# A weight chunk rounded one step later on ScalarE, in the projections of a two-block fp32 transformer kernel

## What is computed

```
h = rms_norm(x, norm1_w[l]) * (1.0 + scale1) + shift1
proj = (h.astype(dt) @ w_in[l]).astype(jnp.float32)
aq, ak, av, gq, gf, gi, gg = jnp.split(proj, split_at, axis=-1)
aq = rope_partial(rms_norm(aq.reshape(hs), q_norm_w[l]), positions)
ak = rope_partial(rms_norm(ak.reshape(hs), k_norm_w[l]), positions)
attn = dilated_attention(aq, ak, av.reshape(hs)).reshape(B, S, ATTN_WIDTH)
ho = hgrn2(gq, gf, gi, lb_all[l])
```

## Time and profile before

| | |
|---|---|
| three runs | 2380.01, 2382.95, 2384.18 us (median 2382.95) |
| the profiled execution | 2381.23 us, of which the profile's span is 2379.1 us |
| TensorE matmul busy | 2318.3 us (97% of the span) |
| TensorE weight load busy | 1934.7 us (81%) |
| VectorE busy | 1642.0 us (69%) |
| ScalarE busy | 1046.5 us (44%) |
| GpSimd busy | 59.8 us (3%) |
| mean granted TensorE clock | 0.992 of full speed |
| `w_hi` (L255) | 392 instructions, 1.917 us each |
| `w_lo` (L259) | 392 instructions, 2.290 us each |

### The profile page before, as it was taken

One profiled execution on the slowest core, in us unless ns is written; L12 is line 12 of the kernel. 1 busy time (PEld: TensorE's weight loads), 2 busy tenths in 40 slices (PEclk: granted clock), 3 DMA queues, 4 the chain that ended last, 5 costly groups with the idle time before them and its releaser, 6 DMA issues.

```text
span 2379.1 us, 27691 instructions
## 1 busy us (share of the span) xinstructions
PE 2318.3 (97%) x10698; PEld 1934.7 (81%) x10698; DVE 1642.0 (69%) x1349; ACT 1046.5 (44%) x922; POOL 59.8 (3%) x56
## 2 busy tenths in 40 slices
PE   4899999999999999999999999999999999999999
PEld 4688888888888888888888888878888888888887
DVE  7969999987677677665578456556665565665665
ACT  2255553436444343343444566664443443443442
POOL 0011000001000000000000011000000000000000
PEclk9789999999999999999999999999999999999999
DMA  9989997754877777666665545445566666666663
GB/s 352 378 299 336 351 338 265 258 204 155 285 250 276 261 266 272 232 227 211 201 223 175 182 155 178 165 142 171 201 225 213 210 228 211 220 220 212 217 224 123
DMA packets 258185, 553.86 MB, mean 233 GB/s; under 512 B 12281, under 2 KB 29122, under 8 KB 255426
## 3 DMA queue, kind: packets, MB, share of 16 engines
q1 hardware_dynamic: 257408, 552.72, 67.3%
q10 hardware_dynamic: 706, 0.17, 0.0%
HBM read 533.96 MB, written 18.87 MB: 232 GB/s over the span
## 4 chain that ended last, share of the span: by engine, by line
PE 92%; DVE 3%; DMA 2%; ACT 1%; DVEq 1%; POOL 0%; issue 0%; SPq 0%; ACTq 0%
PE PS L280 28%; PE PS L282 28%; PE PS L281 28%; DMA ada_raw<-in_w_ada_dram 2%; PE PS L1811 1%; DVE w_lo L259 1%; PE PS L1746 1%; PE PS L272 1%; PE PS L274 1%; PE PS L273 1%; DVE ada_acc L1197 1%; PE PS L330 1%; PE PS L1756 1%; PE PS L1772 0%; POOL rstd L652 0%
## 5 line engine op out<-in xcount | busy, mean ns | idle before, releaser
L259 DVE TENSOR_TENSOR w_lo<-raw,w_hi 128x2048 fp32r<-128x2048 f32 x392 | 897.4, 2290 | 497.1 <-ACT w_hi L255 491.5
L255 ACT ACTIVATE w_hi<-raw 128x2048 fp32r<-128x2048 f32 x392 | 750.9, 1917 | 985.0 <-PE PS L282 954.4
L280 PE MATMUL PS<-w_hi,A_hi 128*128 128x512 f32 x2040 | 807.9, 396 | 3.2 <-DVE A_lo L388 1.9
L282 PE MATMUL PS<-w_hi,A_lo 128*128 128x512 f32 x2040 | 797.5, 391 | 0.0
L281 PE MATMUL PS<-w_lo,A_hi 128*128 128x512 f32 x2040 | 797.1, 391 | 0.0
L280 PEld LDWEIGHTS PS<-w_hi,A_hi 128*128 128x128 f32 x2040 | 385.2, 189 | 82.5 <-DVE A_lo L388 2.0
L282 PEld LDWEIGHTS PS<-w_hi,A_lo 128*128 128x128 f32 x2040 | 384.7, 189 | 81.2
L281 PEld LDWEIGHTS PS<-w_lo,A_hi 128*128 128x128 f32 x2040 | 385.2, 189 | 78.1 <-issue 1.0
L280 PE MATMUL PS<-w_hi,H_hi 128*128 128x512 f32 x1024 | 398.5, 389 | 0.4 <-DVE SQ L1646 0.4
L282 PE MATMUL PS<-w_hi,H_lo 128*128 128x512 f32 x1024 | 398.4, 389 | 0.0
L281 PE MATMUL PS<-w_lo,H_hi 128*128 128x512 f32 x1024 | 398.4, 389 | 0.0
(11 more groups left out here) (274 smaller groups left out, 1216.3 us busy)
## 6 DMA issues: line engine op xcount, KB each, us to landing
raw<-in_w_ff_dram SPq DMA_DIRECT2D x128, 1024.0 KB, 5.3
raw<-in_mlp_w_in_dram SPq DMA_DIRECT2D x64, 1024.0 KB, 5.3
raw<-in_mlp_w_out_dram SPq DMA_DIRECT2D x64, 1024.0 KB, 5.1
raw<-in_w_in_dram SPq DMA_DIRECT2D x56, 1024.0 KB, 8.0
X<-in_w_ada_dram SPq DMA_DIRECT2D x96, 512.0 KB, 5.6
raw<-in_sb_w_qkv_dram SPq DMA_DIRECT2D x48, 1024.0 KB, 5.1
ada_raw<-in_w_ada_dram SPq DMA_DIRECT2D x32, 1024.0 KB, 9.7
raw<-in_w_out_dram SPq DMA_DIRECT2D x16, 1024.0 KB, 6.3
```

Source lines behind the costliest of these rows:

```text
L255: act.activation(w_hi[:, j, :, :], raw[:, j, :, :], ACT.Copy).then_inc(hi_rdy, 1)
L259: dve.tensor_tensor(w_lo[:, j, :, :], raw[:, j, :, :], w_hi[:, j, :, :].bitcast(F32), ALU.subtract).then_inc(lo_rdy, 1)
L280: pe.matmul(bank(pair + t), h, w_hi[:, j, k, :], start=first, stop=False)
L282: mm = pe.matmul(bank(pair + t), l, w_hi[:, j, k, :], start=False, stop=last)
```

## The change

In every step of the four groups ScalarE rounds chunk x+3 in place of chunk x+4, where x is TensorE's chunk of the step: the same chunk that VectorE takes the rest of in that step. The rounding of each chunk so moves from the end of step s-1 to the end of step s, behind step s's part of the previous group and step s's own work. Ahead of the first step one rounding less stands, and behind the last one more. The wait of each rounding (`chunk_done`, the load) is the same as before, and no instruction is added, removed or changed.

```diff
@@ -846,7 +846,6 @@
                 split_hi(act, n // CH, n % CH)
             turn_act(act, 0, g1, mod[:, SHIFT1, :], turned, steps=ALL[4:], first=4, banks=SECOND_STEPS,
                      between={1: lambda: split_hi(act, 2, 0)})
-            split_hi(act, 2, 1)
             groups = proj_groups()
             for i, (kind, idx, B0, nb) in enumerate(groups):
                 for s in range(0 if i else HEAD, CH * nb):
@@ -856,7 +855,7 @@
                     if i == 1:
                         at_own(0, PROJ0, CH * 3 + s)
                     (hg_own if kind == "hg" else at_own)(idx, B0, s)
-                    split_hi(act, B0 + s // CH + 1, s % CH)
+                    split_hi(act, B0 + (s - 1) // CH + 1, (s - 1) % CH)
                     if kind == "hg" and idx == 0 and s == 15:
                         act.wait_ge(rstd_rdy, POWER_OF[1])
                         for c in (0, 1):
@@ -879,6 +878,7 @@
                 act.wait_ge(gate_mm, n + 1)
                 act.activation(dst, bank(4 + b % 2), ACT.Copy).then_inc(gate_rdy, 1)
 
+            split_hi(act, OUT0, CH - 1)
             hg_stage(1, OUT0 - 4, 0)
             for pos in range(OUT_EARLY - 1):
                 for l in OUT_WIDE.get(pos, ()):
```

## The result

| | kernel before | changed kernel |
|---|---|---|
| median, six runs each on one chip | 2382.82 us (2380.01 to 2384.56) | 2392.75 us (2392.13 to 2393.55) |
| ratio, 95% interval | | 1.0045 (1.0035 to 1.0056) |
| profiled execution, span | 2381.23, 2379.1 us | 2392.45, 2390.7 us |
| TensorE's waits, 140 to 560 us | 1.07 | 8.7 |
| VectorE's waits for `w_hi`, 140 to 345 us | 3.3, in 2 | 16.8, in 11 |

The change costs 9.9 us by the medians. The forecast was 2392.

The account below looks back on a forecast made before the run. TensorE and VectorE were both taken as full from 215 to 345 us. VectorE's 11.3 us delay made TensorE 9.6 us late: 2390.8 from the profiled 2381.23, 2392.6 from the median 2382.95; forecast 2392, range 2386.5 to 2397.

Parts of the forecast that it names:

- ten chunks: Chunks 15, 17, 20, 21, 24, 25, 29, 31, 33, 35: VectorE held up by late roundings, 11.3 us by 313 us.
- wait of 215.49: TensorE's existing 1.07 us wait for exponentials: no room there, so VectorE's delay makes it 2.5 us late.
- exponentials near 264: First exponentials of the third group: TensorE loses the rest of the sum, 1.2 us.
- 289.52: Where TensorE turns exponentials: VectorE is 7.05 us late by then, so TensorE loses 1.5 us more.
- 302.12: Where TensorE next turns exponentials, room 1.3 us before: it loses 1.8 us more.
- 363.97: TensorE takes VectorE's second level product, room 1.7 us before: it loses 2.6 us more, 9.6 us late in all.
- short pieces behind its drains and in waits for the norms and for GpSimd, which stay: VectorE's 9.6 us of idle time from 215 to 345 us, claimed unable to take back its delay.
- No change: TensorE binds and `w_lo` is three chunks ahead of use, so 3 us late is in time; 2383 us, chance 0.05.
- Only the first place costs: VectorE finds time between 215 and 345 us; 2.5 us at 215.49 remains, perhaps one later; 2385.5 us, chance 0.07.
- Not slower: First group's head norms start 1.8 us sooner, which removes TensorE's 1.07 us wait at 215.49; 2382 us, chance 0.03.
- The clock falls too: Half-clock stretches follow TensorE's new waits: 2393.5 to 2395 us for one or two, 2399.5 for five; chance 0.13.
- It doesn't do what it says: ScalarE waits for loads, not for TensorE, so they hide the change; given no chance.

Follow-up runs that it names:

- g2_new: Changed order only in the third projection group, all other groups as in the kernel before; 2389.74 us, ratio 1.0033 against the kernel before.
- five_early: Changed kernel, but chunks 15, 25, 31, 33 and 35 rounded ahead of their step's work; 2382.37 against 2381.98 us for the kernel before.
- norm_alone: Kernel before, but VectorE waits for GpSimd's power in each first-block head norm; one run, 2385.93 against 2382.47 us.
- norm_drain: Kernel before plus four VectorE drains between a head norm's sums and `w_lo`, four places in the first block; 2381.59 against 2382.7 us.
- before_lite: Kernel before with the first block's modulation multiply-adds on 64 of 1024 columns; 2382.46 against 2382.47 us.
- g0_new: Changed order in the first group alone, chunk 15 rounded ahead of the second group's first step; 2381.23 against 2382.47 us for the kernel before.
- after_lite: Changed kernel with the first block's modulation multiply-adds on 64 of 1024 columns; 2382.35 against 2382.47 us for the kernel before.
- both_later: Changed kernel with VectorE's `w_lo` one step later too; 2382.19 against 2381.98 us for the kernel before.
- norm_gap: Kernel before plus one VectorE scratch-tile fill between a head norm's sums and `w_lo`, four places in the first block; 2385.17 against 2382.24 us.

## Why the prediction was right

**VectorE's waits.** The sum named ten chunks with 11.3 us of delay together. Chunk 15: `w_lo` at 178.56, plus the 1.46 us by which this profile is late from the start, is 180.02; it stands at 181.85, 1.83 late against 1.81 forecast. (Its idle time of 4.21 us is longer, since VectorE came there earlier than in the kernel before.) Chunk 25: 1.05 against 1.28. Chunk 31: 2.43 against 2.50. Chunk 33: 1.41 against 1.48. Chunk 35: 2.95 against 3.02. Chunks 17, 21 and 29 show no wait, but by the starts of `w_lo` VectorE falls back by 0.18, 0.10 and 0.17 us there, against 0.06 to 0.16 and a hand-over each. Chunk 24 waits 0.34 us against 0.39, and chunk 20, for which the sum had the same, does not wait at all. The method, to take the end of the work that the rounding now stands behind and add 1.92, was good to 0.1 us at four of the five large ones and to 0.25 at chunk 25. g2_new shows that the last three arise by themselves, and five_early that without the five large ones no loss is left. VectorE's delay behind chunk 35 is 10.2 us (313.58 against 301.95, less 1.46) in place of 11.3.

**TensorE's portions.** The start offset of 1.46 taken off, TensorE is late by 1.3 us at 218.22 (before: 215.49), 5.9 at 309.46 (302.12) and 8.5 at 373.96 (363.97). The portions, forecast and measured:

| place | forecast | measured |
|---|---|---|
| wait of 215.49 | 2.5 | 1.3 |
| exponentials near 264 | 1.2 | 1.1 |
| 289.52 | 1.5 | 1.5 |
| 302.12 | 1.8 | 2.0 |
| 363.97 | 2.6 | 2.7 |

**The term that was off** is the first, and in it the step "short pieces behind its drains and in waits for the norms and for GpSimd, which stay". They did not stay. Of VectorE's four waits of 1.2, 1.2, 0.9 and 0.9 us for the scaled projections, the two for QN fell to nothing. There `w_lo` (chunks 11 and 19) was held back for 0.33 and 0.15 us by its rounding, and the power, now first, took 1.97 us less (152.38 and 207.68). The second gave VectorE 0.9 us back, and `w_lo` of chunk 20, behind it, did not wait the forecast 0.39 us: 1.3 us, of which 0.15 went to chunk 19's wait, which the sum had at nothing. That leaves the 1.1 to 1.2 us that are missing; VectorE's delay is 2.3 us at chunk 19 and 1.3 us at chunk 20, where the sum had 2.5. norm_alone and norm_drain show that the power is short when it starts first. The delay that I had counted as cost bought something back.

**How it still came out at 2392.** Forecast from the profiled time 2381.23 + 9.6 = 2390.8, measured for the profiled execution 2392.45. The stage gave 8.6 in place of 9.6. The offset at the start added 1.5 and the clock behind 1576 us another 1.5; neither was in the prediction. Against the medians it is 9.9 for 9.6. That the number is so near is in part luck: the term that was a microsecond too large was offset by time that the prediction had not seen.

**The rivals.** *No change* had the right engine for the kernel before, and before_lite bears it out: TensorE binds there. It fell because TensorE wants VectorE's maxima and products without a chunk's lead. *Only the first place costs* is refuted by g2_new, which loses 7.8 us without it. *Not slower*: the first group's gain exists (the wait of 1.07 us is gone in g0_new), but it decides only if chunk 15 is in time, as said there. *The clock falls too*: behind all seven new waits it stayed at 1.00; behind the one of 2.43 us the row is shown above. *It doesn't do what it says*: the waits for `w_hi` are there.

**The sentence on what bounds** read "two engines are full". That was too strong. With VectorE at 93% and TensorE at 99.6% the first looked like a bound of its own; before_lite took a third off it for nothing. VectorE is an engine without room: in the kernel before nothing is won by relieving it, and most of what it is held up reaches TensorE (10.2 us of delay by chunk 35 became 8.5 us at 373.96). Only the second was in the prediction. Once it is held up the first no longer holds, as after_lite shows.

## What to carry to other kernels

A stage handed from one engine to the next wants a step of distance between producer and consumer more than it wants lead at the end: here TensorE could give up a whole chunk of lead for nothing (both_later), and ScalarE's one step was worth 9.9 us. What decides is what the moved instruction now stands behind, so look for the few steps in which that work is long or itself waits (five of 50), and move the instruction ahead of it there. And to know if a busy engine binds or only has no room, take work off it and time that: the price of delay and the value of relief are not the same number. Take it off in the kernel that you have: it was worth 0.0 us in the kernel before and 10 us in the changed one.

## What the hardware showed that was not expected

**A small GpSimd operation doubles when VectorE is ahead of it.** The 128x8 power takes 1.64 us if it starts first, be it by 0.07 us (207.68 against `w_lo` at 207.75 in the changed kernel), and 3.6 us when a 2.29 us subtraction of two tiles started 0.17 us before it; it then ends 1.5 us after that subtraction. A fill of 0.48 us in front made it 4.09. The Trainium skill, page "SBUF — State Buffer", section "Who interferes with whom", says that a VectorE instruction with two inputs in SBUF contends with a GpSimd instruction that reads SBUF, for a read port that they share. Its section "SBUF: two separate sides" has it that whichever of the two starts first holds the shared ports for the whole instruction. That they contend agrees with the traces; of the second statement only one direction does: `w_lo`, 0.07 to 0.25 us behind the power, kept its 2.29 us and was not held. "Who interferes with whom" counts a fill with VectorE as in contention on the other chip generation only. Here the power came 0.37 us ahead of `w_lo` in norm_gap, a longer lead than those that sufficed, and still ended behind it; the one difference is the fill that was running. Whether it was in the way by a port or otherwise no run tells.

**The same wait, two clocks.** At 1576.52 us TensorE stands 2.03 us for VectorE in the kernel before, at 1586.55 us 2.04 us in the changed one. Behind it the granted clock (busy time by stage, before and then after):

```profile
1576.52:1579.52 3.00, 2.87 (x14) 2.25 (x15) 3.00 (x9) 2.43 (x6) 0.00 (x0) 1.00 0.93 299
```

```profile
1588.13:1591.13 3.00, 3.00 (x8) 2.35 (x8) 2.36 (x7) 2.87 (x5) 0.00 (x0) 0.50 0.58 225
```

The second row is at the lower level, 1.2 GHz; 3 us there are 1.5 us lost. It fell so in the changed kernel's profile and in those of all ten experiments (0.97 on the mean of 1560 to 1620 us), and not in the profiled execution of the kernel before. 1.5 us is about what that execution lies below its median, but it need not be the reason: g0_new's profiled execution has the fall and took 2380.82 us. The wait of 2.43 us at 373.96 was longer and left the clock at 1.00. A forecast made from one profile should be ready for a microsecond or two of this kind.
